# The order of block 1's work on four engines and a DMA queue, and the norm's scaling on VectorE instead of GpSimd

## The reference, cut to what matters

```python
u = rmsnorm(x, norm_mix_g)
q, k, v, pz, ga, gp = split(u @ w_in)          # 768, 768, 768, 768, 1024, 1024
a = attention_branch(q, k, v)                  # 12 heads of 64, 3 groups of 4, dilation 1, 4, 16
p = pool_branch(pz, w_pool_grp, pool_scale)    # trailing means of 2, 4, 8, 16 tokens
merged = sigmoid(ga) * (a @ w_att_out) + sigmoid(gp) * (p @ w_pool_out)
h = x + merged @ w_out
h = h + square(relu(rmsnorm(h) @ w_mlp_in)) @ w_mlp_out
x1 = rmsnorm(h)                                # input of the second block
```

## Time and profile before

| | |
|---|---|
| median of 3 runs | 2802.91 us (2800.89 to 2803.94) |
| the profiled execution | 2801.92 us, of which the span 2800.1 us |
| granted TensorE clock, mean of the span | 0.997 |
| TensorE busy | 99% |
| VectorE busy | 68% |
| ScalarE busy | 49% |
| GpSimd busy | 7% |

### The profile page before, as it was taken

The page is one execution under the profiler, slowest core; times in us unless marked ns, Lnnn a source line. Parts: engine busy times, 40 slices in busy tenths (PEclk is TensorE's granted clock), DMA queues, the critical chain, the costliest instruction groups (busy, mean ns, idle before and its releaser), DMA issues.

```text
span 2800.1 us, 35091 instructions
## 1 busy us (share of the span) xinstructions
PE 2763.9 (99%) x13208; PEld 2258.3 (81%) x13208; DVE 1899.8 (68%) x2657; ACT 1364.5 (49%) x2195; POOL 188.7 (7%) x130
## 2 busy tenths in 40 slices
PE   8999999899999999999999999999999999999998
PEld 7888777678888888888777788888888888888887
DVE  7888565674866667678766524988245866666787
ACT  7333466423645544444455414887123655544452
POOL 0233212100000000000123200000000000000000
PEclk9999999999999999999999999999999999999999
DMA  4333432333344465532311121212123443384442
GB/s 158 106 110 101 166 106 98 129 105 143 127 150 158 151 258 206 183 111 88 136 59 56 46 60 53 61 53 60 46 68 136 147 153 152 135 328 160 155 136 72
DMA packets 99184, 344.71 MB, mean 123 GB/s; under 512 B 10832, under 2 KB 10960, under 8 KB 92752
## 3 DMA queue, kind: packets, MB, share of 16 engines
q1 hardware_dynamic: 97728, 337.83, 34.8%
q10 hardware_dynamic: 1296, 4.72, 0.6%
HBM read 246.04 MB, written 96.47 MB: 122 GB/s over the span
## 4 chain that ended last, share of the span: by engine, by line
PE 79%; DVE 2%; issue 1%; ACT 1%; DMA 1%; POOLq 0%; POOL 0%; SPq 0%; DVEq 0%; ACTq 0%
PE ps L475 20%; PE pa L3348 11%; PE ps L3348 11%; PE ps L3377 9%; PE pa L3377 8%; PE ps L2968 7%; PE pa L475 4%; PE ps L3395 3%; PE ps L3263 2%; PE pa L3088 1%; PE pa L3133 1%; PE pa L3099 1%; DMA k_rraw<-hff 1%; PE ps L3019 0%; PE pa L3059 0%
## 5 line engine op out<-in xcount | busy, mean ns | idle before, releaser
L465 DVE TENSOR_TENSOR w_lo<-w_raw,w_hi 128x1024 fp32r<-128x1024 f32 (+1 forms) x110 | 137.3, 1248 | 252.2 <-ACT w_hi L459 252.2
L459 ACT ACTIVATE w_hi<-w_raw 128x1024 fp32r<-128x1024 f32 (+1 forms) x110 | 112.4, 1023 | 294.0 <-PE ps L475 166.4
L1555 ACT ACTIVATE krh<-k_rraw 128x512 fp32r<-128x512 f32 x192 | 121.1, 631 | 233.0 <-PE ps L3377 113.1
L2490 DVE TENSOR_TENSOR krl<-k_rraw,krh 128x512 fp32r<-128x512 f32 x192 | 132.6, 691 | 133.7 <-ACT krh L1555 133.5
L475 PE MATMUL ps<-a_hi,w_hi 128*128 128x512 f32 x688 | 212.1, 390 | 0.0
L475 PE MATMUL ps<-a_lo,w_hi 128*128 128x512 f32 x688 | 212.0, 389 | 0.0
L475 PE MATMUL ps<-a_hi,w_lo 128*128 128x512 f32 x688 | 212.0, 389 | 0.0
L3348 PE MATMUL pa<-xh,fwh 128*128 128x512 f32 x448 | 174.6, 390 | 0.0
L3348 PE MATMUL ps<-xl,fwh 128*128 128x512 f32 x448 | 174.5, 389 | 0.0
L3348 PE MATMUL pa<-xl,fwh 128*128 128x512 f32 x448 | 174.5, 389 | 0.0
L3348 PE MATMUL pa<-xh,fwl 128*128 128x512 f32 x448 | 174.5, 389 | 0.0
(11 more groups left out here) (441 smaller groups left out, 6726.1 us busy)
## 6 DMA issues: line engine op xcount, KB each, us to landing
k_rraw<-hff SPq DMA_DIRECT2D x224, 256.0 KB, 2.8
w_raw<-wstream SPq DMA_DIRECT2D x110, 512.0 KB, 3.6
hff<-hbuf SPq DMA_DIRECT2D x32, 1024.0 KB, 3.8
wA<-wff SPq DMA_DIRECT2D x16, 2048.0 KB, 8.8
hff<-hbuf SPq DMA_DIRECT2D x32, 768.0 KB, 3.2
w_raw<-wff SPq DMA_DIRECT2D x32, 512.0 KB, 4.3
f_raw<-wff SPq DMA_DIRECT2D x32, 512.0 KB, 4.5
proj<-res SPq DMA_DIRECT2D x24, 512.0 KB, 5.4
```

Source lines behind the costliest of these rows:

```text
L459: nc.scalar.activation(w_hi[:, slot, 0:n], w_raw[:, slot, 0:n], ACT.Copy).then_inc(s_whi, 1)
L465: nc.vector.tensor_tensor(w_lo[:, slot, 0:n], w_raw[:, slot, 0:n], w_hi[:, slot, 0:n].bitcast(F32), ALU.subtract).then_inc(s_wlo, 1)
L1555: nc.scalar.activation(k_r[e % 4][0][:], k_rraw[:, r % 4], ACT.Copy).then_inc(sem("s_khi"), 1)
L2490: nc.vector.tensor_tensor(k_r[e % 4][1][:], k_rraw[:, r % 4], k_r[e % 4][0][:].bitcast(F32), ALU.subtract).then_inc(sem("s_klo"), 1)
```

## The change

The norm's scaling moves: VectorE's `proj_first` now multiplies the bank by `rb` as it evicts it, and VectorE's `proj_scale` multiplies the other three quarters of a pair, 128x512 each; GpSimd's and ScalarE's parts are removed. At the start gate 1 is evicted, made tanh of and stored ahead of gate 0, unit 3 waits for the eviction of gate 1 alone, and the splits of x move on ScalarE. `LAST_ORDER` becomes 1, 4, 5, 0, 6, 2, 3. The weights of units 6 and 7 are loaded ahead of the attention. In the attention steps ScalarE evicts v, then sums the probabilities, makes the exponentials, and only then the pool's and q's and k's splits, the weight split of the unit that ended one step before, and the tanh of the unit that ended four steps before; VectorE makes the row maxima first, evicts the gate, and splits the weights of the unit that ended three steps before. Two of the pool's splits move (`PHI_STEPS` 44 and 48 to 42 and 46, `PLO_STEPS` 45 and 49 to 43 and 47). In the row stage `mixed_lo(0)` is made ahead of the row minima, the split of the weights `U_PO[0]` ahead of `mixed_hi(3)` and `mixed_lo(3)`, the spreading goes from (2, 3), (3, 0), (3, 3), (4, 0) to (3, 0), (3, 3), (4, 0), (4, 3), and in the merge VectorE's order changes, too. The core of the diff:

```diff
@@ -55,7 +55,7 @@
            ("v", 2), ("q", 2), ("k", 2), ("v", 3), ("q", 3), ("k", 3), ("z", 2), ("z", 3),
            ("v", 4), ("q", 4), ("k", 4), ("v", 5), ("q", 5), ("k", 5), ("z", 4), ("z", 5)]
 N_PROJ = len(P_UNITS) // 2
-LAST_ORDER = (1, 4, 5, 6, 0, 2, 3)
+LAST_ORDER = (1, 4, 5, 0, 6, 2, 3)
 PREFILL = 24
 REC_ORDER = (0, 1, 6, 2, 3, 4, 5, 7)
 
...
@@ -639,7 +639,9 @@
             def proj_store(i):
 
                 for o in range(2):
-                    sp.wait_ge(sem("s_pjsc"), 2 * i + o + 1)
+                    if o == 0:
+                        sp.wait_ge(sem("s_pj11"), i + 1)
+                    sp.wait_ge(sem("s_pjsc"), 3 * i + (1 if o == 0 and i < LASTP else 3))
                     sp.dma_start(proj[2 * i + o], proj_out(i)[:, o]).then_inc(sem(f"s_hst{i % 2}"), 16)
 
             def att_load(kind, p, dst, loaded):
@@ -679,7 +681,7 @@
                 load_unit(sp, u, u % 2)
             sp.wait_ge(s_wlo, N_START)
             proj_load(0)
-            for m in range(2):
+            for m in (1, 0):
                 gate_store(m)
             sp.wait_ge(sem("s_Traw"), 3)
...
@@ -698,13 +700,16 @@
             for p in range(2):
                 qk_load(p)
                 v_load(p)
+            load_unit(sp, 6, 0)
             for t in range(2):
                 z_load(t)
             proj_store(LASTP)
+            load_unit(sp, 7, 1)
             for t in range(2, 4):
                 z_load(t)
             for m in range(N_START, N_GATE):
-                load_unit(sp, m + 2, m % 2)
+                if m >= 6:
+                    load_unit(sp, m + 2, m % 2)
                 gate_store(m)
                 if m % 2 and m < 13:
                     p = (m - 1) // 2
```

The attention steps, ScalarE and VectorE:

```diff
 
             return 3 * p + which
 
+        def done_before(s, n):
+
+            return unit_at(1, s - n) if s >= n else None
+
...
                     v_out(n)
                 for s in range(END1):
                     p, q = divmod(s, STEPS_PER_PAIR)
-                    done = unit_at(1, s - 1) if s else None
                     if p + 1 < N_PAIR1 and V_STEP[1] <= q < V_STEP[1] + VB[1]:
                         v_out(VB[1] * (p + 1) + q - V_STEP[1])
-                    if done is not None:
-                        unit_hi(done)
-                    if s in PHI_STEPS:
-                        pool_hi(PHI_STEPS[s])
                     if 2 <= s < NS1 + 2:
                         probs_pair(s - 2)
                     for hh in range(2):
@@ -1139,10 +1117,14 @@
                             exp(2 * s + hh)
                         if hh == 0 and s >= 7 and (s - 7) % 4 == 0:
                             o_out((s - 7) // 4)
+                    if s in PHI_STEPS:
+                        pool_hi(PHI_STEPS[s])
                     if next_operand(s, OP_STEP):
                         first_operand_hi(*next_operand(s, OP_STEP))
-                    if done is not None:
-                        gate_tanh(done)
+                    if done_before(s, 1) is not None:
+                        unit_hi(done_before(s, 1))
+                    if done_before(s, 4) is not None:
+                        gate_tanh(done_before(s, 4))
                 unit_hi(N_GATE - 1)
                 gate_tanh(N_GATE - 1)
...
                                             negate=True).then_inc(s_max, 1)
 
                 for s in range(END1):
-                    done = unit_at(1, s - 1) if s else None
-                    if done is not None:
-                        split_lo(dve, done + 2, done % 2, done + 1)
                     if s < NS1:
                         add_max(2 * s)
                         add_max(2 * s + 1)
-                    if done is not None:
-                        gate_out(done)
+                    if done_before(s, 1) is not None:
+                        gate_out(done_before(s, 1))
+                    if done_before(s, 3) is not None:
+                        m = done_before(s, 3)
```

The scaling on VectorE, and the start on VectorE:

```diff
                 nc.vector.tensor_tensor(proj_half(i, o, c), in_order(i, o, in0), in_order(i, o, p_u2), ALU.add
                                         ).then_inc(sem("s_fc"), 1)
 
+            def proj_first(i, at):
+
+                dve.wait_ge(sem("s_prod1"), 7 * i + at + 1)
+                if i >= 2:
+                    dve.wait_ge(sem(f"s_hst{i % 2}"), 32 * (i // 2))
+                nc.vector.tensor_tensor(proj_half(i, 0, 0), in_order(i, 0, proj_bank(i, 0)),
+                                        in_order(i, 0, rb[:, half(0)]), ALU.mult).then_inc(sem("s_pj11"), 1)
+
+            def proj_scale(i, o, c, made):
+
+                dve.wait_ge(sem("s_fc"), 3 * i + made)
+                x = proj_half(i, o, c)
+                nc.vector.tensor_tensor(x, x, in_order(i, o, rb[:, half(c)]), ALU.mult).then_inc(sem("s_pjsc"), 1)
+
             def proj_p75(i, copied):
 
                 dve.wait_ge(sem("s_pcp"), copied)
@@ -2010,18 +2010,17 @@
             def first_units():
 
                 split_lo(dve, 2, 0, 1)
-                rms(0)
+                rms(0, lambda: t_sum(T1))
                 split_lo(dve, 3, 1, 2)
+                t_lo(T1)
+                gate_out(1)
                 gate_out(0)
-                t_sum(T1)
-                gate_out(1)
+                t_sum(T3)
                 proj_sum(0, 0)
-                t_lo(T1)
-                gate_out(2)
-                t_sum(T3)
-                t_sum(T2)
                 proj_lo(0, 0)
                 proj_lo(0, 1)
+                t_sum(T2)
+                gate_out(2)
                 t_sum(T4)
                 proj_sum(0, 1)
                 proj_lo(0, 2)
```

The start on ScalarE, and the row stage on ScalarE:

```diff
                 split_hi(act, 2, 0, 1, 1)
                 for k in range(4):
                     scaled_input(k)
+                split_hi(act, 3, 1, 1, 2)
+                scaled_input(4)
+                t_hi(T1)
+                for k in range(5, KT):
+                    scaled_input(k)
                 copy_rb(0)
-                split_hi(act, 3, 1, 1, 2)
-                t_hi(T1)
-                for k in range(4, KT):
-                    scaled_input(k)
-                gate_tanh(0)
-                gate_tanh(1)
+                for m in (1, 0):
+                    gate_tanh(m)
                 proj_hi(0, 0)
                 proj_hi(0, 1)
-                gate_tanh(2)
                 t_hi(T3)
                 t_hi(T2)
+                proj_hi(0, 2)
+                proj_hi(0, 3)
                 act.wait_ge(sem("s_gst0"), 16)
                 act.wait_ge(sem("s_gst1"), 16)
                 t_hi(T4)
-                proj_hi(0, 2)
-                proj_hi(0, 3)
+                gate_tanh(2)
                 gate_tanh(3)
                 for n in range(4, 7):
                     proj_hi(0, n)
...
                 act.wait_ge(sem("s_mgd"), 2 * (a + 1))
                 nc.scalar.activation(att1_hi[:, a], og[:, a], ACT.Copy).then_inc(sem("s_ahi"), 1)
 
-            for n in range(3):
-                row_out(n)
+            row_out(0)
             mixed_hi(0)
-            for n in range(3, 6):
-                row_out(n)
+            row_out(1)
+            row_out(2)
             mixed_hi(1)
-            row_exp(0)
-            row_exp(1)
+            row_out(3)
             mixed_hi(2)
-            row_exp(2)
             unit_split(U_PO[0])
-            for i in range(3, 6):
-                mixed_hi(i)
+            mixed_hi(3)
+            row_out(4)
+            mixed_hi(4)
+            for g in range(3):
+                row_exp(g)
+            mixed_hi(5)
+            row_out(5)
```

The row stage on VectorE:

```diff
 
                 link(nc.vector.reciprocal(mmin[:, half(c)], lrow[:, 0, half(c)]))
 
+            mixed_lo(0)
             dve.wait_ge(sem("s_rowc"), 3)
             link(nc.vector.tensor_tensor(mmin[:], mrow[0][:], mrow[1][:], ALU.min))
+            mixed_lo(1)
             link(nc.vector.tensor_tensor(mmin[:], mmin[:], mrow[2][:], ALU.min))
-            mixed_lo(0)
-            for g in range(3):
+            mixed_lo(2)
+            nc.vector.tensor_tensor(mrow[0][:], mrow[0][:], mmin[:], ALU.subtract).then_inc(sem("s_rowd"), 1)
+            unit_split(U_PO[0])
+            mixed_lo(3)
+            for g in (1, 2):
                 nc.vector.tensor_tensor(mrow[g][:], mrow[g][:], mmin[:], ALU.subtract).then_inc(sem("s_rowd"), 1)
-            mixed_lo(1)
-            dve.wait_ge(sem("s_rowc"), 6)
+            mixed_lo(4)
+            dve.wait_ge(sem("s_rowc"), 5)
             for g in range(2):
                 dve.wait_ge(sem("s_rowe"), g + 1)
                 link(nc.vector.tensor_tensor(lrow[:, g], lrow[:, g], mrow[g][:], ALU.mult))
-            mixed_lo(2)
```

More of the change, by code:

```diff
@@ L1059, in projections @@
                             proj_copy(i, n, n)
-                        elif n == 2:
-                            proj_first(i, n)
                         proj_hi(i + 1, n)
@@ L1069, in projections @@
                 first_operand_hi(0, 1)
-                proj_first(i, 5)
                 act.wait_ge(sem("s_prod1"), 7 * N_PROJ)
```

(42 more changed lines are left out.)

54 lines of the change are left out of this document (17 added, 37 removed).

## The result

The changed kernel takes 2810.15 us (median of 13 runs, 2806.16 to 2815.02) against 2802.91 (13 runs, 2800.89 to 2806.62). The ratio is 1.0028, 95% interval 1.0020 to 1.0035: slower by 7.8 us, or 5.6 to 9.8, so just beyond the 0.2% that a measurement can tell. The forecast was 2808, range 2795 to 2822. The profiled execution took 2811.02, its span 2809.2.

What follows compares the result with a forecast made beforehand. TensorE, busy 98.7% of the span, was taken to bound the kernel. Terms -8.2 -0.8 +12.6 +0.2 gave +3.8, so 2806.7 as a median, and later loads made it 2808; range 2795 to 2822.

Steps and rivals of the forecast that it cites:

- later loads: Attention: the second, third and fourth set of loads land 0.3 to 1 us later than the first, together 1.3.
- Part 1: Projections: the norm's scaling moves to VectorE, which stays about as full, and TensorE already runs through; 0 us.
- the cover: Projections: each VectorE split is made a whole pair, 19 us, ahead; without it each 0.7 us would count.
- rival D: Projections: VectorE is not freed and becomes 18 us late, 57 us against 39 of slack; 2821, chance 0.02.
- Part 2: Start: the wait of 2.39 goes, product 2 starts 5.7 us earlier, the slow clock's 2.5 goes; -8.2 us.
- Part 3: End of the projections: product 0 before product 6 in the last pair hides ScalarE's copy; -0.8 us.
- Part 4: Attention: late tanh delays loads behind the gate store; waits plus 9.4, slow clock plus 3.2; +12.6 us.
- rival C: Slower: clock stays down 6.8 us behind each long wait, U_PO[0]'s split costs more, loads later; 2821, chance 0.14.
- Rival A: Attention: the loads are in time, 4.4 us from gate store's issue to v's landing; 2783, chance 0.13.
- Rival B: Attention: v is late but ScalarE's held eviction and new dips overlap it, row stage gains 3; 2799, chance 0.13.
- Part 5: Row stage and merge: first waits shrink, a late weight split delays `mixed_lo(3)`, the late merge split goes; +0.2 us.

Runs made afterwards that it cites:

- `time_gps`: `sp_time` with GpSimd scaling the projected tiles again and the last pair in its old order; 2785.63 us.
- `sp_time`: Changed kernel with SyncE's loads of q, k, v and of unit m + 4's weights ahead of gate_store(m), the tanh unmoved; 2785.11 us.
- `start_only`: Kernel before with only the reordering of the start, GpSimd still scaling; 2795.39 us.
- `time_norow`: `sp_time` with the row stage and merge in their order of before; 2784.21 us.
- `sp_u18`: `sp_time` with the first pool unit's weights loaded ahead of the last gate store; 2783.04 us.
- `recip`: Changed kernel with VectorE's gate product 0 and the weight split of U_PO[2] moved between the two reciprocals; 2807.29 us.
- `best`: `sp_u18` with the edit of `recip`, the split between the reciprocals; 2774.11 us.
- `scale_only`: Kernel before with only the scaling moved to VectorE and the last pair's new order; 2799.84 us.

## Why the prediction was right

The mechanism was right: loads written behind a gate store that waits for a late tanh reach TensorE late, and that costs more than the rest of the change gains. In the two profiled spans the forecast was +5.1 (3.8 by the parts and 1.3 for later loads) and +9.1 came: -9.2 for -9.0 up to the end of the projections, +17.7 for +13.9 in the attention, +0.9 for +0.2 behind it, -0.3 in the rest. The term that was off most is the slow clock in the attention, 10.1 us lost for 4.8. By the medians the difference is 7.2, which looks better, because the profiled execution of the changed kernel lay 0.9 above its median and that of the kernel before 1.0 below. That 2808 came within 2.2 of the median is in part luck.

**Part 1 (0).** Right in time, and the cover was there: 0.5 between `time_gps` and `sp_time`. VectorE's rows of 70 to 300 in the changed kernel, the moved multiplication and the split of the earlier trace rows:

```profile
L1985 DVE TENSOR_TENSOR res<-res,rb 128x512 f32<-128x512 f32 x36 | 30.7, 879 | 0.4
L1962 DVE TENSOR_TENSOR pwl<-p_s,pwh 128x512 fp32r<-128x512 f32 x44 | 30.2, 689 | 33.0 <-ACT pwh L980 33.0
```

The split takes 0.69 in place of 1.18 on average, as forecast. An added multiplication takes 0.88 on average, not the 0.69 I took: 0.68 to 0.69 in the pairs of dilation 1, and about 1.05 in those whose tokens are put in another order on the way (`in_order`). 48 of them cost some 42 us, not 33. But more was given back than the 22 us counted. 1.18 is a mean of two kinds: the median split took 0.69 in the kernel before as well, and what met a GpSimd multiplication took 2.5 to 3.4. VectorE's and GpSimd's timelines of the kernel before, one such pair:

```profile
104.27 2.88 DVE L1976 TENSOR_TENSOR pwl<-p_s,pwh 128x512 fp32r<-128x512 f32 x1
```

```profile
103.90 2.71 POOL L871 TENSOR_TENSOR res<-res,rb 128x1024 f32<-128x1024 f32 x1 [11.74 <-DVE res L1984]
```

From 78 to 290 there were 22 VectorE operations of that length, in several lines and not in the splits of sums alone: some 53 us beyond 0.69 each. So VectorE's busy time in 78 to 290 fell from 173.0 to 159.8, where "about as full" was forecast, and rival D (57 us against 39 of slack) had no ground; its 2821, besides, leaves out the forecast's own 5. The Trainium skill (SBUF — State Buffer, Who interferes with whom) says that VectorE's two-input operations contend with GpSimd's reads of SBUF for a shared port pair, which is an exclusive lock. The trace agrees: the operation that met a GpSimd multiplication of 2.71 was held for about as long. It brought no time, since neither engine was on TensorE's path.

**Part 2 (-8.2).** Product 2 starts at 63.81 behind a wait of 1.70; forecast were 64.0 and 1.5. `start_only` gives -7.6.

**Part 3 (-0.8).** The wait is gone; the projections end 9.2 sooner, forecast 9.0.

**Part 4 (+12.6, and 1.3 for later loads).** The chain was as forecast: tanh, gate store, loads, V batch, then the weights that hold ScalarE. The tanh ends at 333.8. The forecast's 345.9 was on the time axis of the kernel before; less 9.2 for the start and 2.7 for the first eviction's wait that the change took away as well, it is 334.0. The four waits are 3.56, 3.11, 3.53 and 3.07, forecast 3.2 each. The weights took less than forecast: the eviction cost 0.83 and 2.35 on the first and the fourth and nothing on the others, where 0.9 each and 3.5 were counted. In their place came 4.0 on L3149 (3.5 behind the output's eviction, 0.5 issue) where 0.7 was counted, 2.4 of it at 508.16. There the output's eviction comes late on ScalarE: the pool's last split now stands ahead of it (505.41, 1.04 us), and before that an exponential waited 1.26 for the row maximum, which stands on VectorE behind a pool sum that had itself waited 1.06 for GpSimd. That points to the pool's work moved two steps earlier, which I had costed at nothing; it is read from the timelines, and the move was not tried alone. It is the one wait that I missed, and it stays in the best kernel. In sum 20.5 of waits against a forecast of 19.7, or 21.0 with the 1.3 for later loads. The size that was off is the clock: 10.1 us lost in place of 4.8. (By these rows the part comes to 10.2 of waits and 8.5 of clock, 18.7, one more than the landmarks show.) In place of four short dips came three stretches, of 3.5, 7.7 and 14.7 us; the last holds two waits, 3.07 at its start and 2.35 within it. That is rival C's mechanism, partly: some long waits bring the clock down for as long as the 4.84 did or longer, and not each does. Rival A needed 4.4 us from the gate store's issue to V's landing; they were 335.5+6.4-333.8 = 8.1. Rival B would have had the eviction and the dips hidden in each other, and they were not.

**Part 5 (+0.2).** +0.9 in the traces and in `time_norow`. The wait for `mixed_lo(3)` was 2.5 with 0.5 behind it, forecast 3.9; the last was 5.2 with a dip of 1.8 us, forecast 4.8 and 1.6. The third product starts at 564.95 where it was 556.3, 8.6 later, while the whole stage began 8.5 later: "about when it starts now" held. The reason given for it held in part only. The forecast put a delay of 4.4 of VectorE's chain down to the late weights. Counted from the first row transposition the second reciprocal ends at 43.1 where it ended at 35.8, 7.3 later; with the weights in time (`sp_u18`) it ends at 40.1. So 3.0 of the delay are the weights. The other 4.3 are there with the weights in time, and what they cost TensorE goes with another order of VectorE's list (`recip`, `best`).

**The rule on DMA waits.** The Trainium skill (TensorE: Matmul & The Clock Gate, HAM oscillation) says that a DMA wait between short groups of matmuls throws the clock down each time. In the trace of the changed kernel the wait of 3.56 at 342.01 left the clock up, and the other three, of 3.1 to 3.5, brought it down. In `recip`, whose attention is the same program, the wait at the same place did bring it down:

```profile
341.72 0.52 PE L3075 MATMUL pa<-cst,qkv 128*128 128x128 f32 x3 [3.35 <-issue]
...
342.50:346.00 3.50, 3.46 (x12) 2.44 (x11) 0.64 (x2) 1.81 (x3) 0.00 (x0) 0.53 0.00 0
```

So the rule's direction holds, its "each time" does not: the same wait does it in one execution and not in another. The scatter of the changed kernel fits that: over its 13 runs, 8.9 us apart where the kernel before has 5.7, the mean clock goes from 0.996 (2806.16, 2807.67, 2807.69) to 0.992 (2813.32, 2815.02).

## What to carry to other kernels

When an operation moves later on one engine, look at what waits for it on the queue that is strictly in order, and then at everything written behind that waiting entry: here a tanh that nobody needed soon held up the loads that TensorE needed two steps on, and another order of a few lines of the queue was worth 25 us. Take an engine's long chain of small operations (two reciprocals and three products, 10.4 us) apart with the short operation that the bottleneck engine waits for. Before trusting a mean, look at the median and the longest: 1.18 us was no operation's time here. An engine relieved where the bottleneck already runs through gives nothing, whatever its own rows gain.

## What the runs showed of the hardware

Waits of the same length in the same place, in executions of the same instructions, left the granted clock at 2.4 GHz or dropped it to 1.2: 2.39 and 2.40 us at 48 left it up in the profile of before and not in that of `scale_only`, 3.56 and 3.35 at 342 left it up in the changed kernel and not in `recip`. The low stretches were 3.1 to 3.5 us, 6.7 to 7.7, or, with two waits in it, 14.7 long. The cost of such a wait is its length and, in some executions, more: 1.5 to 2.8 us for the stretches shown here that hold one wait, 5.7 for the one that holds two. VectorE operations of 128x512 that met GpSimd's multiplication of 128x1024 took 2.5 to 3.4 us in place of 0.69, about as long as the multiplication itself (2.4 to 4.3). A VectorE multiplication of 128x512 in f32 took 0.68 to 0.69 with tokens in order and 1.03 to 1.10 with tokens reordered.
